# Attention remainders and value splits shared out anew between VectorE and GpSimd

## The chip, the cores and the metric

One core of one Trainium2 chip runs the whole program. The metric is the device time of that core in microseconds (us), the median of three runs. The engines are called TensorE (PE in the rows, its weight loads PEld), VectorE (DVE), ScalarE (ACT), GpSimd (POOL) and SyncE (SP).

## The reference, cut to what matters

The kernel computes one layer of an encoder for a prompt of 2048 tokens and a sample of 256: a mixer whose one half is a long convolution and whose other half is attention, then a mixture of experts. The change lies in attention alone, which computes, for 8 heads with queries and keys of 96 and values of 64:

```python
def attend(q_blk):
    s = jnp.einsum('bqhd,bkhd->bhqk', q_blk, k)
    p = jax.nn.softmax(s, axis=-1)
    return jnp.einsum('bhqk,bkhd->bqhd', p, v)
```

## The kernel before, in words

The stages follow one another: projections, attention (`attend`), the convolution, the merge, the experts. Attention keeps 16-bit precision products but makes each fp32 factor of two 16-bit parts: a rounded part and a remainder. So queries, keys, values and the exponentials of the scores all exist as a pair.

A head of the prompt is 64 **steps**, numbered n = 0 to 63 (`NS`). Each handles 128 keys against a block of 512 queries; 16 steps (`KT`) make a block and 4 blocks (`NQ`) a head. After the 8 heads come 8 steps for the sample, all heads of it together ("short"). For one step:

- TensorE makes the scores with three products (`scores`, lines 1143 to 1145), into one of two PSUM tiles `pS`.
- ScalarE takes the exponential twice: in fp32 (`pf`, line 1092) and rounded to 16 bits (`p1`, line 1093).
- The **remainder** `p2 = pf - p1` is made by `rest` (line 959), a subtraction of two 128x512 operands. For the steps listed in `own` VectorE makes it, for the `others` GpSimd.
- TensorE multiplies `p1` and `p2` by the values (`values`, line 1164), 8 products; they wait for the remainder (`own_done` or `others_done`), and their end frees the step's buffers (`p_free`; four of each).

TensorE's own order is written out in `head`: scores of step n + 3, values of step n, then a piece of the work that leads for the block after the next one, `lead`. That work finds each query's largest score: 16 **slots** per block, each one product (line 1120) into one of two PSUM tiles `pM`, which VectorE reduces (line 1221) and so frees (`pM_free`). It runs 24 steps ahead (`LEAD`). Steps with n % 16 of 0 and 8 have two slots, those of 6 and 7 none; the others one. After the last slot VectorE joins the maxima (`join`, line 1231), TensorE transposes them into `pM[0]` (line 1128, in the step with n % 16 = 7), VectorE moves them out of PSUM (`move`, line 1238), and only then may TensorE make slot 0 of the next block, behind the values of the step with n % 16 = 8 (`max_moved`). SP carries the moved maxima into the queries' extra row.

VectorE and GpSimd both work through the steps in order and do the remainders two steps ahead (`AHEAD`): in body n they first make the remainder of step n + 2, if it is theirs. VectorE then does its slots with join or move, a part of the normalising of the block before (lines 1255 to 1274), and one of 16 pieces of splitting the next head's queries and keys (`split_qk`, lines 1207 and 1210; bodies in `split_at`). GpSimd, after the remainder, splits the next head's values in the bodies listed in `v_split_at`: half of the key tiles, 128x512, first the rounded part (line 1057), then the remainder (line 1059). So the one queue of each engine decides who is late: a value split in body n stands behind the remainder of step n + 2 and in front of that of step n + 3.

Of the kernel before, what the change touches and what calls it, by code (L numbers as in the profile page):

```python
# [13 lines left out]
P = 128  # L14
# [10 lines left out]
NH, ND, QH, VH = 8, 64, 96, 64  # L25
# [800 lines left out]
def mixers(nc, io):  # L826
    with nc.sbuf_tensor("z", [P, NT, CH], F32) as z:
        attend(nc, io, z)
        clear_semaphores(nc)
        hyena(nc, io, z)  # L830


def attend(nc, io, z):
# [6 lines left out]
    NQ, KT, QT = L // QB, L // P, L // P  # L840
    NS = NQ * KT
# [4 lines left out]
    NC = L // CW  # L846
    TQ = QB // P
    VC = 1 + 2 * VH
    VC2 = 1 + VH
    SPLITS, V_SPLITS = 4 * NC, 4  # L850
    KS = LS // P
    NSS = NH // 2 * KS
    assert NH * LS == L and 2 * LS == QB and KS * 2 == TQ
# [16 lines left out]
    split_at = [1, 9, 11, 12, 14, 15, 17, 25, 27, 28, 30, 33, 41, 43, 44, 46]  # L870
    first_split_at = [3, 6, 9, 11, 12]
    second_split_at = [22, 25, 27, 28, 30, 31, 33, 41, 43, 44, 46, 47, 49, 50, 52, 57]
    v_split_at = [5 + 14 * m for m in range(V_SPLITS)]
    norm_at = 2
    own = [n for n in range(NS) if n % KT in (9, 12, 15)]
    others = [n for n in range(NS) if n not in own]
    z_after = ((0, 2), (0, 3), (1, 1))
    z_in_heads = [range(i * NT // 3, (i + 1) * NT // 3) for i in range(3)]
    with ExitStack() as ctx:
        def sb(name, shape, dt=F32):  # L880
            return ctx.enter_context(nc.sbuf_tensor("at_" + name, shape, dt))
# [12 lines left out]
        zero = sb("zero", [P, 1])  # L894
# [16 lines left out]
        qk_in, v_in, split, v_split = sem("qk_in"), sem("v_in"), sem("split"), sem("v_split")  # L911
# [42 lines left out]
        def rest(eng, h, n):  # L954

            r = n % 4
            eng.wait_ge(p_free, NS * h + n + 1)
            eng.wait_ge(pS_free, NS * h + n + 3)
            eng.tensor_tensor(p2[r][:, :], pf[:, r, :], p1[r][:, :], ALU.subtract).then_inc(  # L959
                own_done if n in own else others_done, 1)  # L960

        def rest_ahead(eng, mine, h, n):
            steps = NSS if short(h) else NS
            if n + AHEAD < steps:
                if n + AHEAD in mine:
                    rest(eng, h, n + AHEAD)
            elif not short(h) and n + AHEAD - NS in mine:
                rest(eng, h + 1, n + AHEAD - NS)
# [70 lines left out]
        @block.gpsimd  # L1039
        def _(pool):  # L1040
            pool.memset(zero[:, :], 0.0).then_inc(ready, 1)
            pool.wait_ge(ready, 1)
            for b in range(2):
                pool.memset(k1[b][QH:QH + 1, :], MAX_UNIT).then_inc(ready, 1)
                pool.wait_ge(ready, 2 * b + 2)
                pool.memset(vv[b][:, :, 0:1], 1.0).then_inc(ready, 1)
                pool.wait_ge(ready, 2 * b + 3)

            def split_v(h, b, m):

                step, half = divmod(m, 2)
                tiles = slice(half * KT // 2, (half + 1) * KT // 2)
                parts = vv[b][:, tiles, 1:].rearrange("p k (s d) -> p s k d", s=2)
                pool.wait_ge(v_split, V_SPLITS * h + m - 1) if m >= 2 else pool.wait_ge(v_in, 16 * h + 16)
                nil = zero[:, :].unsqueeze(2).to_broadcast([P, KT // 2, VH])
                if step == 0:
                    ins = pool.tensor_tensor(parts[:, 0, :, :], v[:, tiles, :], nil, ALU.add)
                else:
                    ins = pool.tensor_tensor(parts[:, 1, :, :], v[:, tiles, :], parts[:, 0, :, :], ALU.subtract)
                ins.then_inc(v_split, 1)  # L1060

            def head(h, b):
                for n in range(NS):
                    rest_ahead(pool, others, h, n)
                    if n in v_split_at:
                        if n == v_split_at[0]:

                            pool.wait_ge(p_free, NS * h + 4)
                        split_v(h + 1, 1 - b, v_split_at.index(n))

            for m in range(V_SPLITS):
                split_v(0, 0, m)
            for n in range(AHEAD):
                if n in others:
                    rest(pool, 0, n)
            for h in range(NH):
                head(h, h % 2)
            for n in range(NSS):
                rest_ahead(pool, others, NH, n)
# [1429 lines left out]
```

## Time and profile before

| what | us |
|---|---|
| median of 3 runs (3351.68 to 3358.54) | 3354.52 |
| the profiled execution, its own time | 3351.22 |
| its span on the profile | 3349.4 |
| TensorE busy | 2938.2 (88%) |
| VectorE busy | 1591.5 (48%) |
| ScalarE busy | 1308.5 (39%) |
| GpSimd busy | 1002.2 (30%) |

The shares are means over stages with different limits. Attention's steps run from about 711 to 1385 us. The rows of this stretch give an instruction's start from the beginning of the span, and the time for which it occupied its engine. Products on TensorE are pipelined, so the distance between two starts tells what a product costs, and the shown duration does not.

### The profile page before, as it was taken

Reading aid. Unit: us, or ns where it says so; the run is one execution under the profiler, and the core shown is the slowest. Engines: PE = TensorE matmul, PEld = TensorE weight load, DVE = VectorE, ACT = ScalarE, POOL = GpSimd, SP = SyncE. Lnnn points to the kernel's source line nnn. Section 1 sums busy time; section 2 is a strip of 40 time slices with the busy share of each in tenths; the row PEclk is TensorE's granted clock in tenths of the full one; section 3 lists DMA queues with packets and bytes.
Section 4 is the critical chain, followed back from the end, with each engine's and each line's share of the span. In section 5 each row is a group of like instructions: output and inputs, shape, how many; then the busy total and the mean of one; then the engine's idle time right before and its main releaser. Section 6 shows DMA issues by size and latency. Waiting matters only on the chain. (4 is left out here: it accounts for less than half of the span.)

```text
span 3349.4 us, 39224 instructions
## 1 busy us (share of the span) xinstructions
PE 2938.2 (88%) x14279; PEld 1610.0 (48%) x14279; DVE 1591.5 (48%) x2416; ACT 1308.5 (39%) x2322; POOL 1002.2 (30%) x928
## 2 busy tenths in 40 slices
PE   7999999869999999779868969999009999999998
PEld 4555555535555555423222324454006566566664
DVE  3244444358888888565575543332781111111111
ACT  3333333249999999674345422222001110110100
POOL 0111111148888888650163001111000111111111
PEclk9999999979999999899979979999559999999999
DMA  5112232225111111288858973433403645556551
GB/s 150 40 52 79 79 91 77 68 68 199 33 33 33 33 33 33 67 358 294 282 198 329 308 239 115 134 113 94 161 29 104 188 159 170 161 155 189 168 154 29
DMA packets 245478, 443.73 MB, mean 132 GB/s; under 512 B 54494, under 2 KB 135518, under 8 KB 243616
## 3 DMA queue, kind: packets, MB, share of 16 engines
q1 hardware_dynamic: 187952, 354.89, 31.8%
q0 software_dynamic: 10752, 37.75, 5.4%
q10 hardware_dynamic: 46608, 48.92, 4.5%
q8 instruction: 99, 1.62, 0.2%
q14 instruction: 67, 0.55, 0.0%
HBM read 289.73 MB, written 151.73 MB: 132 GB/s over the span
## 5 line engine op out<-in xcount | busy, mean ns | idle before, releaser
L959 POOL TENSOR_TENSOR at_p<-at_pf,at_p 128x512 f16<-128x512 f32 x424 | 512.8, 1221 | 145.7 <-ACT at_p L1093 122.3
L578 PE MATMUL pj_ps<-pj_xT,pj_wch 128*128 128x512 f32 (+1 forms) x960 | 381.0, 550 | 0.8 <-issue 0.8
L1221 DVE TENSOR_REDUCE at_mxs<-at_pM 128x1 f32<-128x512 f32 x512 | 342.3, 685 | 78.5 <-PE at_pM L1120 67.9
L1092 ACT ACTIVATE at_pf<-at_pS,at_scale 128x512 f32<-128x512 f32 x520 | 358.3, 689 | 39.9 <-PE at_pS L1145 39.8
L1093 ACT ACTIVATE at_p<-at_pS,at_scale 128x512 f16<-128x512 f32 x520 | 355.2, 683 | 0.0
L1164 PEld LDWEIGHTS at_pO<-at_vv,at_p 128*128 128x128 f16 x4160 | 234.2, 98 | 141.0 <-POOL at_p L959 31.9
L2342 ACT ACTIVATE ex_si<-ex_pG 128x288 f32<-128x288 f32 x64 | 26.3, 410 | 660.9 <-PE ex_pG L2369 653.6
L1164 PE MATMUL at_pO<-at_vv,at_p 128*128 128x129 f16 x4160 | 268.3, 207 | 8.3 <-POOL at_p L959 6.4
L2369 PE MATMUL ex_pG<-ex_xT,mo_gate 128*128 128x288 f32 x1024 | 261.9, 410 | 0.6 <-ACT ex_xT L2335 0.6
L578 PEld LDWEIGHTS pj_ps<-pj_xT,pj_wch 128*128 128x128 f32 x960 | 179.4, 190 | 167.7 <-issue 162.4
L2369 PE MATMUL ex_pU<-ex_xT,mo_up 128*128 128x288 f32 x1024 | 258.8, 406 | 0.0
L1973 PE MATMUL mg_pU<-z,mg_yT 128*128 128x512 f32 x576 | 252.1, 596 | 0.2 <-ACT mg_yT L1882 0.2
L2369 PEld LDWEIGHTS ex_pG<-ex_xT,mo_gate 128*128 128x128 f32 x1024 | 194.5, 191 | 65.8 <-issue 13.5
L2381 PE MATMUL ex_pY<-mo_down,ex_hT 128*128 128x512 f32 x512 | 223.1, 594 | 0.7 <-issue 0.7
L2369 PEld LDWEIGHTS ex_pU<-ex_xT,mo_up 128*128 128x128 f32 x1024 | 194.8, 190 | 53.5
L1120 PE MATMUL at_pM<-at_k,at_q 96*128 96x512 f16 x512 | 190.2, 390 | 31.8 <-DVE at_q L1207 16.7
L2296 POOL TENSOR_TENSOR ex_mark<-ex_mark 128x1 f32<-128x1 f32 x64 | 12.1, 189 | 671.8 <-DVE ex_ys L2439 446.9
L1143 PE MATMUL at_pS<-at_q,at_k 97*128 97x512 f16 (+1 forms) x528 | 200.4, 380 | 3.9 <-issue 2.2
L1144 PE MATMUL at_pS<-at_q,at_k 96*128 96x512 f16 (+1 forms) x528 | 200.2, 379 | 0.0
L1145 PE MATMUL at_pS<-at_q,at_k 96*128 96x512 f16 (+1 forms) x528 | 199.0, 377 | 0.0
L2422 DVE TENSOR_TENSOR ex_hT<-ex_si,ex_pU 128x288 f32<-128x288 f32 x64 | 29.1, 454 | 334.7 <-PE ex_pU L2369 333.0
L1634 DVE TENSOR_TENSOR sp_pk<-sp_kk,sp_pX 128x512 f32<-128x512 f32 x152 | 104.6, 688 | 163.3 <-ACT sp_kk L1575 84.7
(240 smaller groups left out, 4251.6 us busy)
## 6 DMA issues: line engine op xcount, KB each, us to landing
sp_rows<-s_F SPq DMA_DIRECT2D x76, 768.0 KB, 6.9
s_F<-fs_a SPq DMA_DIRECT2D x72, 768.0 KB, 4.8
mo_gate<-in_w_gate SPq DMA_DIRECT2D x16, 2048.0 KB, 8.3
mo_up<-in_w_up SPq DMA_DIRECT2D x16, 2048.0 KB, 13.2
mo_down<-in_w_down SPq DMA_DIRECT2D x16, 2048.0 KB, 11.1
s_G<-sp_gg ACTq DMA_DIRECT2D x72, 256.0 KB, 5.8
sp_tab<-tab_spec SPq DMA_DIRECT2D x76, 192.0 KB, 4.5
s_QK<-pj_R ACTq DMA_DIRECT2D x18, 768.0 KB, 4.4
```

The costliest lines, as they stand in the source:

```text
L578: last = pe.matmul(pU[n % 2][:, 0:width], wch[ch % 2][:, k, :], xT[:, k, t0:t0 + width], start=(k == 0), stop=(k == KD - 1))
L959: eng.tensor_tensor(p2[r][:, :], pf[:, r, :], p1[r][:, :], ALU.subtract).then_inc(own_done if n in own else others_done, 1)
L1092: act.activation(pf[:, n % 4, :], pS[n % 2][:, 0:QB], ACT.Exp, scale=scale[:, 0:1])
L1093: act.activation(p1[n % 4][:, :], pS[n % 2][:, 0:QB], ACT.Exp, scale=scale[:, 0:1]).then_inc(pS_free, 1)
L1143: pe.matmul(out, k1[b][:, keys], q1[b][:, queries], start=True, stop=False)
L1144: pe.matmul(out, k1[b][0:QH, keys], q2[b][:, queries], start=False, stop=False)
L1145: last = pe.matmul(out, k2[b][:, keys], q1[b][0:QH, queries], start=False, stop=True)
L1164: last = pe.matmul(pO[qb % 2][:, t // 2, (t % 2) * VC:(t % 2) * VC + cols], part[r][:, t * P:(t + 1) * P], vv[b][:, of_v, 0:cols], start=( ...
L1221: dve.tensor_reduce(mxs[:, j // NC, j % NC:j % NC + 1], pM[j % 2][:, :], AX.X, ALU.max).then_inc(pM_free, 1)
L1973: last = pe.matmul(pU[:, h * 512:(h + 1) * 512], yT[t % 2][:, k, :], w[k][h], start=(k == 0), stop=(k == KD - 1))
L2369: last = pe.matmul(out[f % 2][:, 0:NTOK], w[b][:, k, f * P:(f + 1) * P], xT[:, k, :], start=(k == 0), stop=(k == KD - 1))
L2381: last = pe.matmul(pY[0:n, h * 512:(h + 1) * 512], hT[:, f, starts[c]:starts[c] + n], wd[b][:, f, h * 512:(h + 1) * 512], start=(f == 0), ...
```

## The change

VectorE's remainders are now those of steps with n % 16 of 12 and 15; the steps with n % 16 of 9 go to GpSimd, so that a head has 8 on VectorE and 56 on GpSimd (12 and 52 before). The next head's values are split in eight pieces of 4 key tiles, 128x256 each (four of 128x512 before), in bodies 10, 13, 23, 26, 29, 39, 42, 45 (5, 19, 33, 47 before). A remainder piece waits for the rounded piece of the same tiles, four pieces before it.

```diff
-    SPLITS, V_SPLITS = 4 * NC, 4
+    SPLITS, V_SPLITS = 4 * NC, 8
...
-    v_split_at = [5 + 14 * m for m in range(V_SPLITS)]
+    v_split_at = [10, 13, 23, 26, 29, 39, 42, 45]
     norm_at = 2
-    own = [n for n in range(NS) if n % KT in (9, 12, 15)]
+    own = [n for n in range(NS) if n % KT in (12, 15)]
...
             def split_v(h, b, m):
 
-                step, half = divmod(m, 2)
-                tiles = slice(half * KT // 2, (half + 1) * KT // 2)
+                step, quarter = divmod(m, 4)
+                tiles = slice(quarter * KT // 4, (quarter + 1) * KT // 4)
                 parts = vv[b][:, tiles, 1:].rearrange("p k (s d) -> p s k d", s=2)
-                pool.wait_ge(v_split, V_SPLITS * h + m - 1) if m >= 2 else pool.wait_ge(v_in, 16 * h + 16)
-                nil = zero[:, :].unsqueeze(2).to_broadcast([P, KT // 2, VH])
+                pool.wait_ge(v_split, V_SPLITS * h + m - 3) if m >= 4 else pool.wait_ge(v_in, 16 * h + 16)
+                nil = zero[:, :].unsqueeze(2).to_broadcast([P, KT // 4, VH])
```

## Rows read from the trace of the kernel before

**Rows 1.** Stretches: length, busy PE, PEld, DVE, ACT, POOL, PEclk, DMA; heads 4, 7.

```profile
1049.05:1131.20 82.15, 80.20 (x774) 47.50 (x772) 69.81 (x121) 78.21 (x129) 67.11 (x57) 1.00 0.14 33
...
1295.49:1376.21 80.72, 78.22 (x779) 47.93 (x778) 63.03 (x113) 77.29 (x129) 67.08 (x57) 1.00 0.04 8
```

**Rows 2.** Timeline of TensorE, step in head 2 without a wait: start, us, instruction.

```profile
877.42 0.38 PE L1145 MATMUL at_pS<-at_q,at_k 96*128 96x512 f16 x1
877.64 0.51 PE L1164 MATMUL at_pO<-at_vv,at_p 128*128 128x129 f16 x8
877.99 0.38 PE L1120 MATMUL at_pM<-at_k,at_q 96*128 96x512 f16 x1
878.21 0.38 PE L1143 MATMUL at_pS<-at_q,at_k 97*128 97x512 f16 x1
...
878.86 0.51 PE L1164 MATMUL at_pO<-at_vv,at_p 128*128 128x129 f16 x8
```

**Rows 3.** Timeline of TensorE, head 4, steps 7 and 8.

```profile
1058.26 0.27 PE L1128 MATMUL at_pM<-at_eye,at_mx 128*4 128x128 f32 x1
...
1058.81 0.38 PE L1145 MATMUL at_pS<-at_q,at_k 96*128 96x512 f16 x1
1059.47 0.52 PE L1164 MATMUL at_pO<-at_vv,at_p 128*128 128x129 f16 x8 [0.28 <-POOL at_p L959]
1060.26 0.59 PE L1120 MATMUL at_pM<-at_k,at_q 96*128 96x512 f16 x2 [0.27 <-issue]
```

**Rows 4.** Timeline of TensorE, head 4, steps 22 and 24.

```profile
1077.21 0.38 PE L1145 MATMUL at_pS<-at_q,at_k 96*128 96x512 f16 x1
1077.98 0.52 PE L1164 MATMUL at_pO<-at_vv,at_p 128*128 128x129 f16 x8 [0.39 <-POOL at_p L959]
...
1080.22 0.51 PE L1164 MATMUL at_pO<-at_vv,at_p 128*128 128x129 f16 x8
1081.00 0.59 PE L1120 MATMUL at_pM<-at_k,at_q 96*128 96x512 f16 x2 [0.27 <-issue]
```

**Rows 5.** Timeline of TensorE, head 4, step 50.

```profile
1113.60 0.38 PE L1145 MATMUL at_pS<-at_q,at_k 96*128 96x512 f16 x1
1114.11 0.52 PE L1164 MATMUL at_pO<-at_vv,at_p 128*128 128x129 f16 x8
```

**Rows 6.** Timeline of GpSimd, head 4, before step 8's remainder.

```profile
1057.08 1.22 POOL L1057 TENSOR_TENSOR at_vv<-at_v,at_zero 128x512 f16<-128x512 f32 x1
```

**Rows 7.** Timeline of GpSimd, head 4, remainders of steps 50 to 56.

```profile
1112.90 8.03 POOL L959 TENSOR_TENSOR at_p<-at_pf,at_p 128x512 f16<-128x512 f32 x7
```

**Rows 8.** Timeline of VectorE, head 4, around the first move.

```profile
1058.37 1.59 DVE L959 TENSOR_TENSOR at_p<-at_pf,at_p 128x512 f16<-128x512 f32 x1 [0.16 <-PE at_pO L1164]
1059.88 0.27 DVE L1238 TENSOR_SCALAR at_nmx<-at_pM 4x128 f16<-4x128 f32 x1
```

**Rows 9.** Groups of instructions by form, attention: busy and mean, idle before.

```profile
L959 POOL TENSOR_TENSOR at_p<-at_pf,at_p 128x512 f16<-128x512 f32 x424 | 512.8, 1221 | 145.7 <-ACT at_p L1093 122.3 <-PE at_pO L1164 16.5
...
L959 DVE TENSOR_TENSOR at_p<-at_pf,at_p 128x512 f16<-128x512 f32 x96 | 83.1, 865 | 29.9 <-PE at_pO L1164 16.6 <-ACT at_p L1093 11.9
...
L1059 POOL TENSOR_TENSOR at_vv<-at_v,at_vv 128x512 f16<-128x512 f32 x18 | 20.8, 1159 | 0.0
L1057 POOL TENSOR_TENSOR at_vv<-at_v,at_zero 128x512 f16<-128x512 f32 x18 | 20.1, 1120 | 7.2 <-DMA at_v<-s_V 7.2
```

**Rows 10.** Timeline of VectorE, head 4, the cast in body 30.

```profile
1089.90 1.33 DVE L1207 CAST at_q<-at_q 96x512 f16<-96x512 f32 x1
```

**Rows 11.** Timeline of TensorE, head 4, the second slot of step 32.

```profile
1090.98 0.38 PE L1120 MATMUL at_pM<-at_k,at_q 96*128 96x512 f16 x1
1091.88 0.39 PE L1120 MATMUL at_pM<-at_k,at_q 96*128 96x512 f16 x1 [0.53 <-DVE at_mxs L1221]
```

**Rows 12.** Timeline of head 4, two exponentials of ScalarE in a row.

```profile
1058.73 0.70 ACT L1093 ACTIVATE at_p<-at_pS,at_scale 128x512 f16<-128x512 f32 x1
1059.30 0.70 ACT L1092 ACTIVATE at_pf<-at_pS,at_scale 128x512 f32<-128x512 f32 x1
```

## The prediction

> **What bounds the kernel now.** I read the page first, then the busy time by stretch, one stretch per head, because the change touches attention alone. The reader is to see two things in [rows 1]. First, TensorE is busy 80.20 us of a head of 82.15 us, at the full clock (1.00, the 2.4 GHz level); heads 1 to 6 are within 0.02 us of this one, so what is found in head 4 counts six times, and head 7 (80.72) is a near relative. Second, nobody else is full: VectorE 69.8, GpSimd 67.1. ScalarE shows 78.2, but its instructions overlap: started back to back, one follows the other after 0.57 us [rows 12], so two for each of 64 steps need 128 x 0.57 = 73 us. It is no bound at anything that this change can reach.
>
> So the end of attention is set by TensorE's stream and by the places where it stands still. How much is that? A step without a wait is 1.22 us from values to values; the eight products of values take 0.35 us of it, and a slot 0.22 [rows 2]. A block has 12 steps with one slot, 2 with two and 2 with none: 12 x 1.22 + 2 x 1.44 + 2 x 1.00 = 19.52 us, a head 78.1, and with four transposes of some 0.1 us each 78.5. The head takes 82.15, so TensorE waits 3.65 us in it. That is all there is to win: 29 us over 8 heads.
>
> The timeline of TensorE then says where it waits. Without a wait, values start 0.22 us after the last score product [rows 2]. Against that:
>
> - Step 8: 0.66 instead of 0.22, a wait of 0.44 for GpSimd's remainder; then the next slot starts 0.79 after the values instead of 0.35, another 0.44 [rows 3].
> - Step 22: 0.77 instead of 0.22, so 0.55, for GpSimd; step 24: 0.78 instead of 0.35, so 0.43, before the slot [rows 4].
> - Step 50: 0.51 instead of 0.22, so 0.29 [rows 5].
> - Step 32: two slots 0.90 apart instead of 0.22, so 0.68, for VectorE's reduction [rows 11].
>
> These make 2.83 us. The 0.82 left of 3.65 is small change, at steps 23, 40 and 56 and at the transposes; I count 0.45 of it as being of the first two kinds, and that is a choice.
>
> **Why it waits there, and what the change does about each.** The waits for remainders follow a value split. In body 5 GpSimd makes the remainder of step 7, then a split of 1.22 us, and only then, at 1058.3, the remainder of step 8 [rows 6], which the values of step 8 want; the same after the splits of bodies 19 and 47. GpSimd doesn't catch up soon: seven remainders behind each other take 8.03 us, 1.15 each [rows 7], against a step of 1.22. The split of body 33 hits no wait, since TensorE has just stood still for 0.68 us itself.
>
> The change puts no split at bodies 5, 19 and 47. Six of the eight new ones (bodies 10, 13, 26, 29, 42, 45) stand in a body in which VectorE makes the remainder, when GpSimd has a whole step of 1.22 us free. The price of a quarter split isn't in the trace. It lies between half of 1.04 to 1.22, 0.52, and the whole: the two forms have means of 1.12 and 1.16 [rows 9]. I take 0.62, near the half, since the same instruction has half the elements. At 0.62 it costs nothing in a free step of 1.22; that cover would be gone only at 1.22. So the three waits go: 0.44 + 0.55 + 0.29 = 1.28 us a head.
>
> The waits before the slot are another matter. In body 7 VectorE must first make the remainder of step 9, then move the maxima. The transpose starts at 1058.26 and is over some 0.27 later, at 1058.53 [rows 3]; VectorE has by then begun the remainder, which takes 1.59 us, and moves at 1059.88 [rows 8]. TensorE's slot comes at 1060.26. With n % 16 = 9 given to GpSimd, nothing stands between transpose and move: the move would run from about 1058.6 to 1058.9, while the values of step 8 come at 1059.03 at the earliest and last until 1059.38. The move is hidden, and the wait goes: 0.44 + 0.43 = 0.87 us at steps 8 and 24. With the 0.45 counted of the small change, the gross gain is 1.28 + 0.87 + 0.45 = 2.60 us a head.
>
> What is late next? GpSimd gets 4 remainders more, at its own mean of 1.22 us [rows 9]: 4.9 us, and the splits go from four of 1.14 to eight of 0.62, 0.4 more. It was busy 67.1 us; now 72.4 of about 80, 90%. In a block that is 14 x 1.22 + 2 x 0.62 = 18.3 us of 19.6: it keeps up on the mean. It doesn't in two places, after the splits of bodies 23 and 39. Those have no free step: remainder 25, split, remainder 26 come directly after each other, where TensorE's steps are shortest (no slot in steps 22 and 23). So remainder 26 starts some 0.6 us late. How much of that is free? A split of 1.22 us cost TensorE 0.44 at step 8, one of some 1.1 cost 0.55 at step 22 [rows 3, 4, 6, 9], so 0.55 to 0.8 of lateness is absorbed: about as much as is needed. Any remainder that had to wait for VectorE's use of the same memory (mean 1.22 against 1.15 back to back) comes on top. I put 0.25 us of new wait on each of the two places, bounds 0 and 0.6.
>
> VectorE loses 4 remainders that cost it 1.59 us or less each, mean 0.87 [rows 9]: 3.5 us a head. It has idle time, so this alone gains nothing beyond the move. Its cast in body 30 took 1.33 us [rows 10] and made step 32's wait. It stays at body 30, with a split now before it on GpSimd's queue (body 29). I take the wait of 0.68 as staying, bounds 0 and twice that; 0.2 us on the sum for its growing.
>
> Here the Trainium skill has a rule (SBUF — State Buffer, section "SBUF: two separate sides"): a VectorE instruction with two SBUF inputs or in a two-port mode and a GpSimd instruction exclude each other for the whole length of whichever began first. The trace agrees as far as it goes: a remainder on VectorE of 0.87 us mean reached 1.59 with GpSimd's beside it [rows 8, 9]. By the rule, a GpSimd that is busier by 8 points makes VectorE's casts and subtractions wait more often, which speaks against this change. The page on GPSIMD Engine Reference, section "4.1 Engine selection", also advises VectorE for elementwise work, at about twice the speed; the rows say 1.22 against 0.87 us, and what would count by the page, 4 instructions made slower, adds nothing where GpSimd has room.
>
> **The sum.** Per head 2.60 - 2 x 0.25 - 0.2 = 1.9 us. Times 8 is 15 us. Head 0 (more waits, but many from VectorE's own load) and head 7 I count like the rest. The 8 steps of the sample and the splits before the first step, which lie before any remainder, change nothing. From the profiled execution's own time: 3351.2 - 15 = 3336.2 us; the median of the runs lies 3.3 us above that execution, and the prediction is set against the median: 3354.5 - 15 = 3339.5 us. The stages after attention start when it ends, so nothing of it is covered. A difference under 0.2% (6.7 us) can hardly be told from none here.
>
> **Rivals.**
>
> - *The wait moves to GpSimd's new queue.* If a quarter split costs nearly a whole one (1.04), remainders 26 and 42 start over 1 us late and TensorE waits 0.6 to 1.0 at each; 2.60 - 2.0 leaves 0.6 a head, 5 us: 3349.5. For it: GpSimd recovers 0.07 us a step. Against it: half the elements.
> - *Step 32's wait goes too.* The cast waited because it met a running remainder; its phase will be another one. Gain 1.9 + 0.9 = 2.8 a head, 22 us: 3332.
> - *VectorE becomes late, and the kernel slower.* GpSimd fills the steps in which VectorE used to run its casts and subtractions beside an idle GpSimd; each that meets a running GpSimd instruction may be as late as the cast of body 30 and hold up two slots by 0.68 [rows 10, 11]. With the 1.9 that I count on, this decides from three more such waits a head (2.0); with four, one in each block, 4 x 0.68 = 2.7, the head is 0.8 longer, and the kernel 6.6 longer, 3361; more with five. This is what the skill's rule of exclusion would do here. Against it: VectorE idles 12 us of a head, has 3.5 less to do, and pieces of 0.62 hold it up less than those of 1.1.
> - *The move isn't what slot 0 waited for.* Then only the 1.28 and a part of the small change are won: 1.28 - 0.7 + 0.3 = 0.9 a head, 7 us: 3347.5. The rows speak against it, since the slot starts 0.11 us after the move's end.
>
> **How the numbers follow.** My forecast gets 0.55 (own range 3333 to 3346), the larger gain 0.13, the moved wait 0.14, the idle move 0.08, the slower kernel 0.10. The forecast's upper edge, the first two, and half of the idle-move case are faster by over 0.2%: 0.72. Within 0.2%: 0.19. Slower: 0.09. The range is 3329 to 3352: its lower end is the larger gain with no new wait (2.60 + 0.68 = 3.3 a head, 26 us), its upper end takes in the moved wait; left out is the slower kernel and little else.
>
> **What would show it.** In the profile after, heads 1 to 6 should be 80.2 us long (79.5 to 81.2). The move should start less than 0.1 us after the transpose's end in each block, and the next slot right behind the values. TensorE should not wait for GpSimd at steps 8, 22 and 50, and somewhat at 26 or 27 and 42 or 43. The quarter splits should show 0.5 to 0.7 us. GpSimd busy about 72 us a head, VectorE about 66. I would be wrong if VectorE's casts and subtractions grow, with waits of slots on VectorE's reductions at more steps than 32, or if quarter splits cost 1 us.

## The result and the profile after

The kernel became slower: 3370.41 us against 3354.52, medians of five runs each; the ratio is 1.005, with a 95% interval of 1.0035 to 1.0065. I had forecast 3339.5, with a range of 3329 to 3352. The sign was wrong. The ratios, here and below, compare executions at a mean granted clock of about 0.94; one of the ten of the run "even pieces" took 11219.6 us at 0.49 and is left out of its ratio (without it, its median is 3352.4).

The profiled execution after took 3368.09 us, 16.9 more than the one before. Attention, from 711 to 1385 us before and from 710 to 1397 after, is 13 longer and begins 1 earlier. Another 5 lie behind it (1964.4 us became 1969.2), in stages whose code is the same; I have no cause for them, and in the profiles below that part lies anywhere from 1964 to 1973 us, without any pattern.

Busy time by stretch, heads 0, 3, 4 and 7 of the kernel after (length, PE, PEld, DVE, ACT, POOL, granted clock, DMA); it answers to [rows 1]:

```profile
710.46:803.94 93.48, 85.45 (x782) 49.67 (x781) 79.75 (x125) 79.01 (x130) 75.13 (x65) 0.97 0.38 133
...
972.34:1055.15 82.81, 80.09 (x773) 47.76 (x772) 70.73 (x117) 78.15 (x129) 76.46 (x65) 1.00 0.14 33
1055.15:1139.51 84.36, 81.63 (x774) 48.32 (x773) 70.72 (x117) 78.14 (x129) 76.42 (x65) 0.98 0.13 33
...
1306.68:1388.57 81.89, 78.00 (x780) 48.42 (x779) 62.86 (x109) 77.11 (x129) 76.27 (x65) 1.00 0.04 8
```

Head 3 is 82.8 us long where 80.2 was forecast, and head 4 is 84.4. VectorE was to become less busy, about 66 us; it shows 70.7, with four remainders fewer than before. GpSimd was to show 72 and shows 76.5. Something made the instructions of both longer.

First, what did come true. TensorE and VectorE at the first change of block in head 4:

```profile
1064.37 0.27 PE L1128 MATMUL at_pM<-at_eye,at_mx 128*4 128x128 f32 x1
...
1064.91 0.38 PE L1145 MATMUL at_pS<-at_q,at_k 96*128 96x512 f16 x1
1065.13 0.51 PE L1164 MATMUL at_pO<-at_vv,at_p 128*128 128x129 f16 x8
1065.48 0.60 PE L1120 MATMUL at_pM<-at_k,at_q 96*128 96x512 f16 x2
```

```profile
1064.67 0.28 DVE L1238 TENSOR_SCALAR at_nmx<-at_pM 4x128 f16<-4x128 f32 x1 [0.36 <-PE at_pM L1128]
```

The move starts 0.03 us after the transpose's end. The values of step 8 come 0.22 us after the last score product and the slot 0.35 after the values: neither of the two waits of 0.44 us in [rows 3] is left. The same holds at steps 22, 24 and 50.

The loss has one main place, before the values of step 31. TensorE in head 4:

```profile
1093.97 0.38 PE L1145 MATMUL at_pS<-at_q,at_k 96*128 96x512 f16 x1
1096.45 0.53 PE L1164 MATMUL at_pO<-at_vv,at_p 128*128 128x129 f16 x8 [2.10 <-DVE at_p L959]
...
1097.83 0.63 PE L1145 MATMUL at_pS<-at_q,at_k 96*128 96x512 f16 x1
1098.26 0.86 PE L1164 MATMUL at_pO<-at_vv,at_p 128*128 128x129 f16 x8
```

2.48 us pass where 0.22 do without a wait, so 2.26 are lost, and the row says for whom: VectorE's remainder of step 31. VectorE in the 9 us up to it, and GpSimd beside it:

```profile
1087.65 1.30 DVE L1210 TENSOR_TENSOR at_k<-at_k 96x512 f16<-96x512 f32 x1
1088.88 1.10 DVE L959 TENSOR_TENSOR at_p<-at_pf,at_p 128x512 f16<-128x512 f32 x1
1089.90 1.27 DVE L1221 TENSOR_REDUCE at_mxs<-at_pM 128x1 f32<-128x512 f32 x2
1091.09 1.55 DVE L1210 TENSOR_TENSOR at_k<-at_k 96x512 f16<-96x512 f32 x1
1092.57 0.68 DVE L1221 TENSOR_REDUCE at_mxs<-at_pM 128x1 f32<-128x512 f32 x1
1093.17 1.66 DVE L1210 TENSOR_TENSOR at_k<-at_k 96x512 f16<-96x512 f32 x1
1094.76 1.63 DVE L959 TENSOR_TENSOR at_p<-at_pf,at_p 128x512 f16<-128x512 f32 x1
```

```profile
1086.13 2.27 POOL L959 TENSOR_TENSOR at_p<-at_pf,at_p 128x512 f16<-128x512 f32 x2
1088.36 1.06 POOL L1057 TENSOR_TENSOR at_vv<-at_v,at_zero 128x256 f16<-128x256 f32 x1
1089.39 2.71 POOL L959 TENSOR_TENSOR at_p<-at_pf,at_p 128x512 f16<-128x512 f32 x2
1092.07 1.10 POOL L1059 TENSOR_TENSOR at_vv<-at_v,at_vv 128x256 f16<-128x256 f32 x1
1093.13 4.27 POOL L959 TENSOR_TENSOR at_p<-at_pf,at_p 128x512 f16<-128x512 f32 x3
```

GpSimd has no pause from 1086 to 1097. Of VectorE's instructions the reductions, which read PSUM, keep their 0.68 us. The subtractions of two operands in SBUF, which can take 0.7, take 1.10 to 1.66. Five of them follow each other here (splits of bodies 25, 27, 28, remainders 28 and 31), and VectorE never idles between them. GpSimd's own rows stretch too: two remainders in 2.71, where back to back they take 2.3 [rows 7].

Over the whole of attention, first the groups of VectorE whose operands lie in SBUF, then the value splits (shortest, median and longest in ns):

```profile
L1210 DVE TENSOR_TENSOR at_k<-at_k 96x512 f16<-96x512 f32 x32 | 43.7, 1366 | 0.0
...
L1265 DVE TENSOR_SCALAR at_rec<-at_rec,at_v_back 128x4 f32<-128x4 f32 x35 | 28.2, 805 | 0.0
```

```profile
L1057 POOL TENSOR_TENSOR at_vv<-at_v,at_zero x36: 606/1062/1492, 686.6 to 1339.9; 128x256 f16<-128x256 f32 x36
L1059 POOL TENSOR_TENSOR at_vv<-at_v,at_vv x36: 646/1108/1446, 688.9 to 1366.8; 128x256 f16<-128x256 f32 x36
```

The first two had means of 807 and 488 ns before. The product of 128x4 is the plainest: 0.21 us at the least, so a mean of 0.8 us for four columns is waiting. A quarter split is 0.61 or 0.65 us when left alone, as taken (0.62). In head 4 only two of the eight were left alone, those of bodies 23 and 39, the two without a free step. Those of bodies 26 and 29 waited for VectorE's pieces of bodies 25 and 27 and took 1.06 and 1.10. The other four, in bodies 10, 13, 42 and 45, took 1.39 to 1.49 beside a cast and a remainder of VectorE. The one of body 10 on GpSimd, and VectorE beside it:

```profile
1067.94 1.49 POOL L1057 TENSOR_TENSOR at_vv<-at_v,at_zero 128x256 f16<-128x256 f32 x1
```

```profile
1067.94 0.41 DVE L1207 CAST at_k<-at_k 96x512 f16<-96x512 f32 x1
1068.27 0.68 DVE L959 TENSOR_TENSOR at_p<-at_pf,at_p 128x512 f16<-128x512 f32 x1
```

The eight make 9.2 us where 5.0 were forecast; that is GpSimd's 76.5 in place of 72.4.

The stand has a second price. Granted clock of TensorE around it in head 4:

```profile
1090.00:1094.00 4.00, 3.85 (x37) 2.25 (x36) 4.00 (x5) 3.69 (x7) 4.00 (x4) 1.00 0.01 2
1094.00:1097.00 3.00, 0.88 (x10) 0.38 (x8) 3.00 (x4) 1.46 (x3) 2.95 (x3) 1.00 0.01 3
1097.00:1101.00 4.00, 3.95 (x17) 1.88 (x18) 2.81 (x5) 1.27 (x2) 1.49 (x2) 0.57 0.01 4
1101.00:1104.00 3.00, 3.00 (x34) 1.93 (x33) 2.21 (x5) 2.78 (x5) 1.43 (x2) 1.00 0.00 0
```

TensorE was busy 0.88 of 3 us; then 0.57 was granted over 4 us, so most of it at the 1.2 GHz level. Heads 1, 2, 4 and 6 have a mean clock of 0.98 and are 84.0 to 84.5 us long; heads 3 and 5 keep 1.00 and are 82.8. So it costs 1.2 to 1.6 us where it comes. Head 7 has the stand and keeps its clock too.

Head 0, which has its own list of bodies for the pieces (41, 43, 44 and 46 among them), has the same stand before the values of step 47, where the kernel before has none:

```profile
779.96 0.71 PE L1164 MATMUL at_pO<-at_vv,at_p 128*128 128x129 f16 x8 [2.09 <-DVE at_p L959]
```

It is as long, 2.25 us, with pieces of 1.55 and 1.65 us and a remainder of 1.63 in front of it, and a granted clock of 0.57 over the 4 us from 780 on. Head 0 became 2.2 us longer.

### The profile page after: what moved, and what is told of

Its sections match the earlier page's. It is cut to its first block and busy times, and to the rows that moved or that the text cites. A ratio compares the mean times of both kernels' runs of the same rounds, so it can differ in the third digit from the quotient of the medians.

```text
span 3366.2 us, 39260 instructions
## 1 busy us (share of the span) xinstructions
PE 2939.6 (87%) x14279; PEld 1611.4 (48%) x14279; DVE 1599.8 (48%) x2384; ACT 1308.8 (39%) x2322; POOL 1076.1 (32%) x996
## 5 line engine op out<-in xcount | busy, mean ns | idle before, releaser
L959 POOL TENSOR_TENSOR at_p<-at_pf,at_p 128x512 f16<-128x512 f32 x456 | 552.7, 1227 | 85.3 <-ACT at_p L1093 75.9
L1221 DVE TENSOR_REDUCE at_mxs<-at_pM 128x1 f32<-128x512 f32 x512 | 340.5, 683 | 88.1 <-PE at_pM L1120 80.8
```

Source lines behind the costliest of these rows:

```text
L1221: dve.tensor_reduce(mxs[:, j // NC, j % NC:j % NC + 1], pM[j % 2][:, :], AX.X, ALU.max).then_inc(pM_free, 1)
```

## The experiments

The theories, in the words of the expectations. **Theory 1**: VectorE's SBUF instructions each wait for a running GpSimd instruction, and the waits add up in bodies 25 to 31. **Theory 2**: GpSimd simply has too much to do. **Theory 3** (added for the second group): VectorE's own queue is too long there, whatever GpSimd does. Each run was timed beside the kernel before on the same chip; "head" is the usual length of heads 2 to 6 in the profile.

| run | median us | ratio to before (95%) | head us | lost at step 31 |
|---|---|---|---|---|
| after | 3370.4 | 1.005 (1.0035 to 1.0065) | 82.8 or 84.4 | 2.26 |
| own only | 3360.0 | 1.002 (1.001 to 1.003) | 82.7 | 1.24 |
| splits only | 3353.2 | 0.9999 (0.9989 to 1.0008) | 81.8 | 1.28, in head 1 0.16 |
| two splits later | 3363.4 | 1.0026 (1.0016 to 1.0036) | 82.2, one 84.0 | 1.28, in that one 2.24 |
| VectorE's pieces later | 3362.7 | 1.0019 (1.0008 to 1.0029) | 81.8 to 83.8 | 0 |
| two remainders cut | 3349.3 | 0.9983 (0.9974 to 0.9993) | 80.9 | 0 |
| even pieces | 3353.3 | 0.9998 (0.9988 to 1.0008) | 81.3 | 0 |
| before, even pieces | 3367.1 | 1.0041 (1.0027 to 1.0056) | 83.8 | 0 |
| splits only, even pieces | 3353.3 | 1.0003 (0.9994 to 1.0013) | 81.6 | 0 |
| placed pieces | 3351.7 | 0.9992 (0.9983 to 1.0001) | 81.0 | 0 |
| placed, half splits | 3350.4 | 0.9989 (0.998 to 0.9998) | 80.3 to 83.6 | 0 |
| placed, free steps | 3345.1 | 0.9972 (0.9962 to 0.9983) | 80.3 | 0 |
| none in bodies 46, 47 | 3340.3 | 0.9952 (0.9939 to 0.9966) | 79.2 | 0 |

The last column is for heads 1 to 7. In head 0 the stand before step 47 is 2.25 us in "after", "two splits later", "VectorE's pieces later", "two remainders cut" and "even pieces", none of which touch head 0's pieces, and 1.24 to 1.28 in the two halves and in "splits only, even pieces". The forecasts of the first two groups, down to "splits only, even pieces", take no account of it. Theory 1's ranges held the times of "splits only" and of the last run. Eight other times lay above their ranges, and "placed, free steps" below its own; "placed, half splits" had two readings, told below.

**Each half of the change alone.**

```diff
-    own = [n for n in range(NS) if n % KT in (9, 12, 15)]
+    own = [n for n in range(NS) if n % KT in (12, 15)]
```

> The kernel before with one half of the change: steps with n % 16 of 9 go to GpSimd, the value splits stay four of 128x512 at bodies 5, 19, 33, 47. Theory 1 (in the changed kernel VectorE's subtractions in bodies 25 to 31 meet a GpSimd that never pauses there, because a split stands in bodies 26 and 29; each waits for GpSimd's instruction, and remainder 31 ends 3 us late): no split stands near body 28, so remainder 31 is at most 1 us late, the waits at the move (0.87 us a head) go, those for remainders at steps 8, 22 and 50 stay: 3348, range 3342 to 3356. Theory 2 (four more remainders are simply too much for GpSimd): the loss is here already, 3362 or more, with GpSimd busy over 74 us a head.

```diff
-    own = [n for n in range(NS) if n % KT in (12, 15)]
+    own = [n for n in range(NS) if n % KT in (9, 12, 15)]
```

> The changed kernel with VectorE's twelve remainders back: only the eight quarter splits at the new bodies. Theory 1: the two splits in bodies 26 and 29 are still there, but GpSimd skips remainder 25 and comes to body 26 on time; a part of the late remainder 31 stays, 0.5 to 1.5 us a head, against 1.3 us of waits won at steps 8, 22 and 50: 3350, range 3342 to 3362. Theory 2: GpSimd has no more remainders than before, and the gain of the three waits comes whole: 3344.

Neither half alone gives the loss of the whole; moving the remainders costs 0.2%, moving the splits nothing. In both, step 31 stands 1.24 to 1.28 us and step 32 another 0.96. In the first, GpSimd was 71.2 us busy in head 3, below the 74 that theory 2 wanted, and 3360.0 lies above theory 1's range and below theory 2's 3362. But I had expected at most 1 us of lateness in the first without a split near body 28, so theory 1 as I had put it, with the two splits as the cause, was too narrow.

The halves also tell what took the waits away. In "own only" the waits before the slots of steps 8 and 24 are gone, and those for remainders at steps 8, 22 and 50 stay. In "splits only" the waits for remainders are gone, and the one before the slot of step 8 too, though VectorE still makes remainder 9 ahead of the move; 0.15 is left at step 24. VectorE in head 4 of "splits only":

```profile
1057.76 0.69 DVE L959 TENSOR_TENSOR at_p<-at_pf,at_p 128x512 f16<-128x512 f32 x1 [0.16 <-PE at_pO L1164]
1058.37 0.27 DVE L1238 TENSOR_SCALAR at_nmx<-at_pM 4x128 f16<-4x128 f32 x1
```

The remainder took 0.69 instead of 1.59 [rows 8].

**GpSimd's side: two splits moved away.**

```diff
-    v_split_at = [10, 13, 23, 26, 29, 39, 42, 45]
+    v_split_at = [10, 13, 23, 39, 42, 45, 58, 61]
```

> The changed kernel with two of the eight splits moved: those of bodies 26 and 29 go to 58 and 61, all else the same, so that GpSimd's work in a head is the same to the instruction. Theory 1: GpSimd pauses at remainders 28 and 31, the stand of 2.3 us before the values of step 31 goes in every head, and with it the half clock behind it: 3340, range 3334 to 3348. Theory 2: the same work, so the same loss: 3365 to 3372.

Both expectations missed: 3363.4. The stand shrank from 2.26 to 1.28 and did not go, and a wait of 0.96 came before the second slot of step 32, where the changed kernel has 0.08. VectorE in head 4 of this run:

```profile
1088.84 1.56 DVE L1210 TENSOR_TENSOR at_k<-at_k 96x512 f16<-96x512 f32 x1
1090.32 0.68 DVE L1221 TENSOR_REDUCE at_mxs<-at_pM 128x1 f32<-128x512 f32 x1
1090.92 0.67 DVE L1210 TENSOR_TENSOR at_k<-at_k 96x512 f16<-96x512 f32 x1
1091.52 1.64 DVE L959 TENSOR_TENSOR at_p<-at_pf,at_p 128x512 f16<-128x512 f32 x1
```

GpSimd came out of a pause of 1.06 us at 1090.91, within 0.01 us of the start of the split of body 28; the split was not kept waiting and took 0.67. In head 2 of the same run GpSimd's remainder began 0.06 us ahead of it; there the split took 1.64, the stand was 2.24 and the head 84.0 us long. So less than a tenth of a microsecond decides. The split of body 27 and remainder 31 still met GpSimd's remainders. So the splits on GpSimd made about 1 us of the stand; the rest are its remainders, which are there before and after. Of a head they made 0.6 us (82.2 for 82.8).

**VectorE's side: its pieces later.**

```diff
-    split_at = [1, 9, 11, 12, 14, 15, 17, 25, 27, 28, 30, 33, 41, 43, 44, 46]
+    split_at = [1, 9, 11, 12, 14, 15, 17, 33, 35, 36, 41, 43, 44, 46, 49, 51]
```

> The changed kernel with GpSimd's work and places untouched; of VectorE's 16 pieces of queries and keys the three of bodies 25, 27 and 28 (the subtractions of keys) and those after them go later: bodies 33, 35, 36, 41, 43, 44, 46, 49, 51. Theory 1: the collision has two sides, so taking VectorE's side away helps too: remainder 31 is at most 1 us late, 3345, range 3338 to 3355, unless the pieces collide with GpSimd's splits of bodies 39 to 45 in their turn, which would show as waits at steps 42 to 48. Theory 2: nothing changes for GpSimd, 3365 to 3372.

The stand at step 31 went, and another of the same size came in its place. TensorE and VectorE in head 4:

```profile
1106.53 0.27 PE L1128 MATMUL at_pM<-at_eye,at_mx 128*4 128x128 f32 x1 [2.02 <-DVE at_mx L1231]
```

```profile
1104.04 1.64 DVE L1210 TENSOR_TENSOR at_k<-at_k 96x512 f16<-96x512 f32 x1
1105.60 0.68 DVE L1221 TENSOR_REDUCE at_mxs<-at_pM 128x1 f32<-128x512 f32 x1
1106.31 0.17 DVE L1231 TENSOR_REDUCE at_mx<-at_mxs 128x4 f32<-128x16 f32 x1
```

The pieces of bodies 33 and 35 took 0.68, but that of body 36, behind the normalising and ahead of the join of the maxima, took 1.64, and a product of 128x4 in the normalising 1.19. It isn't enough to move the pieces anywhere. 3362.7 lies above theory 1's range and just under theory 2's 3365, so this run doesn't separate the two.

**GpSimd cut, VectorE untouched.** This separates theories 1 and 3. Only 4 of 512 columns of the remainders of steps 29 and 30 are made.

```diff
-            eng.tensor_tensor(p2[r][:, :], pf[:, r, :], p1[r][:, :], ALU.subtract).then_inc(
+            w = 4 if not short(h) and n in (29, 30) else QB
+            eng.tensor_tensor(p2[r][:, 0:w], pf[:, r, 0:w], p1[r][:, 0:w], ALU.subtract).then_inc(
```

> The changed kernel, but GpSimd makes only 4 of 512 columns of the remainders of steps 29 and 30 in each head (the rest of those two remainders is left out, so the attention's output is not the reference's). VectorE's queue, TensorE's and ScalarE's work are untouched. Theory 1 (VectorE's subtractions of bodies 25, 27, 28 and its remainders 28 and 31 each wait for a GpSimd instruction that is running): with GpSimd idle there the subtractions of bodies 27 and 28 take about 0.7 us instead of 1.6, remainder 31 is ready before TensorE wants it, heads 1 to 6 come down from 82.8 and 84.4 to about 80 us: 3340, range 3334 to 3348. Theory 3 (VectorE's own queue is too long in bodies 25 to 31, whatever GpSimd does): the stand before the values of step 31 stays over 1 us in each head: 3360 or more.

VectorE in head 4 (its lines are one higher in this kernel):

```profile
1085.52 0.67 DVE L1211 TENSOR_TENSOR at_k<-at_k 96x512 f16<-96x512 f32 x1
1086.12 0.67 DVE L1222 TENSOR_REDUCE at_mxs<-at_pM 128x1 f32<-128x512 f32 x1
1086.72 0.67 DVE L1211 TENSOR_TENSOR at_k<-at_k 96x512 f16<-96x512 f32 x1
1087.32 0.67 DVE L960 TENSOR_TENSOR at_p<-at_pf,at_p 128x512 f16<-128x512 f32 x1
```

1.55, 1.66 and 1.63 us became 0.67 each, 2.8 us less, by cutting two instructions of another engine to four columns. The stand is gone and head 4 takes 80.8 instead of 84.4. Theory 3 is out. The kernel missed its range (3349 instead of 3348 at most); a wait of 0.9 at step 32, one of 0.57 at step 48 and head 0's stand remain.

**Even pieces, on three kernels.**

```diff
-    split_at = [1, 9, 11, 12, 14, 15, 17, 25, 27, 28, 30, 33, 41, 43, 44, 46]
+    split_at = [1, 5, 9, 12, 15, 17, 21, 25, 28, 31, 33, 37, 41, 44, 47, 49]
```

> The changed kernel with VectorE's 16 pieces of queries and keys spread evenly over a head (heads 1 to 7: bodies 1, 5, 9, 12, 15, 17, 21, 25, 28, 31, 33, 37, 41, 44, 47, 49 in place of 1, 9, 11, 12, 14, 15, 17, 25, 27, 28, 30, 33, 41, 43, 44, 46), none at a body in which it moves the maxima or normalises. GpSimd's queue is untouched. Theory 1: with at most two instructions that exclude GpSimd's in any two bodies the waits don't add up to a step; the stand at step 31 goes, heads 1 to 6 take 79 to 81 us: 3340, range 3333 to 3350. Theory 2 (GpSimd is overloaded on the mean): 3365 to 3372. Theory 3: the same as theory 1, since VectorE's queue is evened too.

> The kernel before with VectorE's 16 pieces spread as in the run above, and nothing else changed. Theory 1: the waits for GpSimd after its value splits and the waits at the move stay (2.6 us a head), the wait of 0.68 at step 32 goes: 3349, range 3344 to 3354.

> The eight quarter value splits at the new bodies, twelve remainders on VectorE as before, and VectorE's 16 pieces spread as above. Theory 1: waits for remainders at steps 8, 22 and 50 gone, the wait at the move stays (0.9 to 1.2 a head), the stand at step 31 gone: heads 1 to 6 about 80.5 us: 3342, range 3336 to 3350. If the move's wait is what counts, this is 7 us slower than the run with eight remainders on VectorE; if VectorE's help counts, it is the faster one.

On the kernel after, this takes back the whole loss, with GpSimd's queue untouched: theory 2 is out. It gains no more than that, because the pieces of bodies 5, 21 and 37 stand ahead of the join, which comes 0.68 us late in the first and 0.95 and 0.98 in the others; head 0's stand remains too. TensorE in head 4:

```profile
1058.98 0.27 PE L1128 MATMUL at_pM<-at_eye,at_mx 128*4 128x128 f32 x1 [0.51 <-DVE at_mx L1231]
```

On the kernel before, the same edit lost 0.4% where I had expected 0.2% gained: it adds the late joins, and GpSimd's half splits at bodies 5, 19 and 47 still delay remainders, 0.85 us at step 8 and again at step 24. With twelve remainders on VectorE and the new splits a head is 0.3 us longer than with eight, and the medians are the same, 3353.3: VectorE's help in step 9 is worth about as much as the move behind it costs, and not 7 us less.

**Pieces placed by what was learnt.**

```diff
-    split_at = [1, 9, 11, 12, 14, 15, 17, 25, 27, 28, 30, 33, 41, 43, 44, 46]
-    first_split_at = [3, 6, 9, 11, 12]
-    second_split_at = [22, 25, 27, 28, 30, 31, 33, 41, 43, 44, 46, 47, 49, 50, 52, 57]
+    split_at = [1, 9, 11, 12, 14, 15, 17, 25, 28, 31, 33, 41, 43, 46, 47, 49]
+    first_split_at = [3, 6, 9, 11, 14]
+    second_split_at = [22, 24, 25, 27, 28, 30, 31, 33, 41, 44, 46, 47, 49, 57, 58, 59]
```

> The changed kernel with VectorE's pieces placed by what the last four runs showed: not in consecutive bodies around its remainders 28 and 31, and not in bodies 5, 21 and 37, where the evenly spread ones held up the joining of the maxima by 0.65 to 0.95 us. Heads 1 to 7: bodies 1, 9, 11, 12, 14, 15, 17, 25, 28, 31, 33, 41, 43, 46, 47, 49; head 0: 22, 24, 25, 27, 28, 30, 31, 33, 41, 44, 46, 47, 49, 57, 58, 59 for head 1's, and 3, 6, 9, 11, 14 for its own last ones. Theory 1 (waits of VectorE for GpSimd, and where they fall, make the whole difference): heads 1 to 6 at 79 to 80 us, head 0 at 94 or less in place of 95.6: 3337, range 3331 to 3345. If the joins' waits come back by another piece: 3350.

> The run above with GpSimd's two value splits of bodies 23 and 39, the only ones with no free step, moved to 58 and 61. Theory 1: GpSimd is late at remainder 26 and 42 no more, but these waits were small on TensorE (0.1 us); 0 to 4 us faster than the run above.

> VectorE's pieces and remainders as in the first run of this group, but the value splits stay four of 128x512, placed in bodies 10, 26, 42 and 58, each in a step of which VectorE makes the remainder. If a half split of 1.04 to 1.13 us fits a free step of 1.22 us as well as a quarter of 0.61 to 0.65 does, this is within 3 us of the run with eight; if VectorE's waits for the longer instruction tell, it is 3 to 8 us slower.

The first reached 3351.7 and not 3337; a wait of 1.2 us stayed at step 48, behind the pieces of bodies 46 and 47, and in head 1 one of 2.1 at step 4. The second, `v_split_at = [10, 13, 26, 29, 42, 45, 58, 61]`, is the first kernel that is clearly faster than before, 9 us, and gained more over the first (7 us) than I had given it. The third, four half splits at 10, 26, 42 and 58, is 5 us slower than the second, but as fast as the first: it is cut up by single waits, one of 0.96 at step 44 with the familiar pair in front of it, a piece of 1.63 and a remainder of 1.64 us.

TensorE's wait at step 48 in the second, there in heads 1 to 5 but not in head 6, which takes 79.0 us:

```profile
1101.80 0.38 PE L1120 MATMUL at_pM<-at_k,at_q 96*128 96x512 f16 x1
1103.22 0.39 PE L1120 MATMUL at_pM<-at_k,at_q 96*128 96x512 f16 x1 [1.04 <-DVE at_mxs L1221]
```

**The last one takes this wait away.**

```diff
-    split_at = [1, 9, 11, 12, 14, 15, 17, 25, 28, 31, 33, 41, 43, 46, 47, 49]
+    split_at = [1, 9, 11, 12, 14, 15, 17, 22, 25, 28, 31, 33, 38, 41, 44, 49]
```

> The best kernel so far (value splits in bodies 10, 13, 26, 29, 42, 45, 58, 61), with VectorE's pieces of heads 1 to 7 moved once more, so that none stands in bodies 46 and 47, ahead of the two slots of step 48: 1, 9, 11, 12, 14, 15, 17, 22, 25, 28, 31, 33, 38, 41, 44, 49. Theory 1: the wait of 1.2 us at step 48 goes; the pieces of bodies 22 and 38 stand between join and move, where VectorE has over 1 us free, and cost 0 to 0.5 us each: heads 2 to 5 at 79.2 us (78.6 to 80.3) after 80.3; 3338, range 3332 to 3346.

Heads 2 and 4 in this run:

```profile
883.05:962.22 79.17, 79.17 (x773) 47.75 (x772) 67.49 (x117) 78.05 (x129) 76.52 (x65) 1.00 0.15 35
...
1041.56:1120.74 79.18, 79.17 (x773) 47.75 (x772) 67.49 (x117) 78.05 (x129) 76.52 (x65) 1.00 0.15 35
```

As expected: 79.2 us, and 3340.3, 30 us below the changed kernel with the same instructions of the same shapes, and 13 below the kernel before. GpSimd is just as busy as after the change, 76.5 us, and TensorE waits for it but once in a head, 0.16 us before the values of step 24. TensorE is busy all of the head; 78.5 is what I had counted for a head without waits.

## Why the prediction was wrong

*What bounds the kernel* held: TensorE's stream and its waits. The last run took away 3.0 of the 3.65 us of waiting in a head.

*The gross gain*, 2.60 us a head, was there. The waits for remainders at steps 8, 22 and 50 and those before the slots of steps 8 and 24 are gone, by the mechanisms named. That the move waited for remainder 9 was right too, but "splits only" shows what made that remainder long: with the splits moved it takes 0.69 us, and the 0.87 us at the slots fall to 0.15 without giving it away. So moving the remainders added little to the gain.

*The price of a quarter split*, 0.62 us, was right for one left alone (0.61 and 0.65). It was used as if it were always left alone. The "free step" of GpSimd is a step in which VectorE makes a remainder, and so a place in which a split meets VectorE in the same memory: six of eight did, and took 1.06 to 1.49. The upper bound, the price of a whole one (1.12 and 1.16 on the mean, 1.22 in [rows 6]), was passed by the four of 1.39 to 1.49. In heads 1 to 7 none of them made TensorE wait.

*What is late next* is the step that failed: "It has idle time, so this alone gains nothing beyond the move", and the 0.2 us put on step 32. VectorE's idle 12 us are a sum over a head. In bodies 25 to 31 it has none: three pieces, five slots and two remainders, and five of these instructions exclude GpSimd's. I had looked for lateness on GpSimd's queue, put 0.25 us on each of two places, and nothing came there: the values of steps 26 and 42 start 0.22 us after the scores. On VectorE's queue I had looked at one instruction, the cast of body 30. What came was 2.26 us at step 31, 0.7 before the slots of steps 28, 30 and 31 together, 0.57 at step 48, and 1.2 to 1.6 us for the clock in four heads of six. The cast of body 30 took 0.41 instead of 1.33, and the wait of 0.68 at step 32, which I had taken as staying and growing, fell to 0.08. Head 3 adds up: 2.6 and 0.6 us gained, 3.9 lost with some 0.3 of small waits, 0.65 longer.

*The rivals.* The third, "VectorE becomes late, and the kernel slower", is what happened, for the reason that it gave; I had given it one in ten. Its price, four waits of 0.68 us, was near the sum and wrong in kind: one chain of five waits, not four single ones. What it named against itself, VectorE's idle time and its 3.5 us less of work, was the error: work that VectorE gave up in bodies 7, 23, 39 and 55 doesn't help in bodies 25 to 31. The Trainium skill has the rule of exclusion (SBUF — State Buffer, section "SBUF: two separate sides"): of a VectorE instruction with two SBUF inputs or in a two-port mode and a GpSimd instruction, whichever starts first has the shared pair of ports for its whole length, and the other is blocked. I had quoted it and then priced it as a remainder of a remainder. The trace after agrees: no slot's reduction, which reads PSUM, took over 0.69 us, and each of VectorE's 73 subtractions of over 0.75 us ended 0.54 to 0.55 us after the end of the GpSimd instruction that ran when it began; with GpSimd idle none took over 0.69.

*Why the kernel before escaped* can be read in part. VectorE's subtraction of body 27 in head 4 of the kernel before, and GpSimd beside it:

```profile
1085.90 0.71 DVE L1210 TENSOR_TENSOR at_k<-at_k 96x512 f16<-96x512 f32 x1
```

```profile
1084.91 2.72 POOL L959 TENSOR_TENSOR at_p<-at_pf,at_p 128x512 f16<-128x512 f32 x2 [1.93 <-ACT at_p L1093]
```

It began 0.17 us before the first of these remainders ended, in every head, and hardly waited. After the change it began 1.01 us before the end of one, and took 1.55. "Splits only" shows both in one kernel: in head 1 it began 0.44 us before, and step 31 stood 0.16; in heads 2 to 7 it was 1.04, and 1.27. The order of the instructions is the same in all of them. So the phase between the two queues decides how long the stand is. What sets the phase is open: the old kernel's waits at steps 22 and 24 may, but no run changes them alone.

## What to carry to other kernels

When two engines exclude each other in a memory, idle time on either is no room: count, body by body, how many such instructions follow each other without a pause while the other engine runs, and price each at the other's whole instruction. Here five in a row made 2.3 us of standing out of 0.7 us instructions. A step in which one of the two engines makes the remainder isn't a free step for the other. And when an edit takes away waits, look at what the waits had kept apart; moving the small pieces of work, with no instruction added, was worth 30 us against the changed kernel, 13 against the one before.

## What the runs showed of the hardware

- A product of 128x4 on VectorE took 0.21 us at the least and had a mean of 0.8 us in attention: behind a GpSimd instruction, its length is mostly that of the other's rest. The profile shows such waiting as busy time, on both engines; the sign of it here is a growing duration for the same shape.
- In the kernel after, VectorE's subtractions waited for one GpSimd instruction at most, 1.66 us in all; none was kept out by two of GpSimd's remainders, which would be 2.3 us. The other way round it isn't so: a split of GpSimd that waited took 1.49 us over a cast and a remainder of VectorE, one after the other.
- A stand of 2.25 us of TensorE was followed by a granted clock of 0.57 to 0.58 over 4 us in heads 1, 2, 4 and 6 of the kernel after, and of 1.00 in heads 3, 5 and 7, with the same instructions in front of it. What decides between them the runs don't show.
- On GpSimd, left alone, a subtraction or addition of 128x256 took 0.61 to 0.65 us, one of 128x512 1.03 to 1.15.
